# Two mixers of a transformer kernel in another order: pooling last, output tiles in two parts, mask and maximum in one operation

## The reference

```python
h = rms_norm(x, mix_norm[l]) @ w_in[l]              # 1024 -> 2304 columns
u_pool = h[..., OFF_POOL:OFF_MOBA]                  # 256 columns
qm, km, vm = split(h[..., OFF_MOBA:OFF_DIL], 3)     # 4 heads of 64 each
qd, kd, vd = split(h[..., OFF_DIL:OFF_CONV], 3)     # 4 heads of 64 each
u_conv = h[..., OFF_CONV:]
y_pool = pool_mixer(u_pool, pool_w[l], pool_scale[l])  # means over 2, 4, 8, 16 tokens, less the token
y_moba = moba_attention(rope(qm), rope(km), vm)     # 256 tokens are one block: causal attention
y_dil  = dilated_attention(rope(qd), rope(kd), vd)
y_conv = conv_module(u_conv, ...)                   # gate, 31 taps by channel, layer norm, silu
x = x + concat([y_pool, y_moba, y_dil, y_conv]) @ w_out[l]
```

## Time and profile before

| | before |
|---|---|
| median of 3 runs | 1927.93 us (1921.69 to 1929.28) |
| the profiled execution | 1923.98 us |
| its span, first to last instruction | 1922.2 us |
| TensorE busy (PE) | 1884.9 us, 98% |
| VectorE busy (DVE) | 1281.9 us, 67% |
| ScalarE busy (ACT) | 916.0 us, 48% |
| GpSimd busy (POOL) | 247.9 us, 13% |
| DMA | 323.78 MB, mean 168 GB/s |
| mean granted TensorE clock | 0.995 of full speed |
| share of the chain that ended last | PE 78%, DVE 14%, ACT 4% |

### The profile page before, as it was taken

How to read it: one execution, slowest core, us unless ns; L and a number is a source line. 1 busy time by engine, 2 the same in 40 slices (tenths; PEclk the granted TensorE clock), 3 DMA queues, 4 the chain that set the end, 5 groups by cost and what they waited for, 6 DMA issues and landing times.

```text
span 1922.2 us, 28534 instructions
## 1 busy us (share of the span) xinstructions
PE 1884.9 (98%) x11790; PEld 1621.2 (84%) x11790; DVE 1281.9 (67%) x1666; ACT 916.0 (48%) x1288; POOL 247.9 (13%) x175
## 2 busy tenths in 40 slices
PE   9999999999999999999999999999999999979998
PEld 7888969887888888888889878988888889679997
DVE  6776796776677669777664564755554367857774
ACT  5334565334533555633464265533333255855554
POOL 0000007732757600000000110000000000000000
PEclk9999999999999999999999999999999999989999
DMA  8675436776577643776452221323223223025552
GB/s 312 254 272 210 176 135 244 278 264 222 204 270 271 229 162 108 269 281 245 154 187 88 110 78 67 110 88 121 88 88 110 91 85 132 12 88 176 176 197 88
DMA packets 50960, 323.78 MB, mean 168 GB/s; under 512 B 5472, under 2 KB 9744, under 8 KB 12816
## 3 DMA queue, kind: packets, MB, share of 16 engines
q1 hardware_dynamic: 39024, 270.09, 38.9%
q10 hardware_dynamic: 10080, 39.28, 5.4%
q0 software_dynamic: 1728, 12.58, 1.7%
HBM read 320.86 MB, written 1.07 MB: 167 GB/s over the span
## 4 chain that ended last, share of the span: by engine, by line
PE 78%; DVE 14%; ACT 4%; issue 2%; DMA 0%; ACTq 0%; DVEq 0%; SPq 0%
PE ps L558 76%; DVE s_wl L1948 5%; DVE s_tmp L2047 3%; ACT s_wh L1275 2%; DVE s_xx L1948 2%; DVE s_big L2247 1%; PE ps L917 1%; DVE s_tmp L2065 1%; PE ps L774 0%; PE ps L751 0%; DMA s_raw<-in_ffn_gate 0%; ACT s_big L1447 0%; DVE s_big L2070 0%; DVE s_tmp L2469 0%; DVE s_X L2445 0%
## 5 line engine op out<-in xcount | busy, mean ns | idle before, releaser
L558 PE MATMUL ps<-s_xx,s_wh 128*128 128x512 f32 (+1 forms) x3328 | 894.0, 347 | 1.4 <-DVE s_wl L2018 0.6
L1948 DVE TENSOR_TENSOR s_wl<-s_raw,s_wh 128x2048 fp32r<-128x2048 f32 x213 | 493.6, 2319 | 287.7 <-ACT s_wh L1275 287.7
L558 PE MATMUL ps<-s_xx,s_wl 128*128 128x256 f32 (+1 forms) x2208 | 668.6, 303 | 0.4 <-DVE s_xx L2472 0.4
L558 PEld LDWEIGHTS ps<-s_xx,s_wh 128*128 128x128 f32 x3328 | 579.9, 190 | 88.6 <-issue 5.7
L1275 ACT ACTIVATE s_wh<-s_raw 128x2048 fp32r<-128x2048 f32 x213 | 403.7, 1906 | 112.8 <-PE ps L558 108.0
L558 PEld LDWEIGHTS ps<-s_xx,s_wl 128*128 128x128 f32 x2208 | 419.0, 190 | 18.8 <-issue 2.7
L558 PE MATMUL ps<-s_wh,s_hl 128*128 128x512 f32 (+1 forms) x608 | 232.6, 383 | 2.9 <-DVE s_tmp L2047 2.4
L558 PE MATMUL ps<-s_wh,s_hh 128*128 128x512 f32 (+1 forms) x608 | 230.3, 379 | 0.0
L558 PE MATMUL ps<-s_wl,s_hh 128*128 128x512 f32 (+1 forms) x608 | 230.3, 379 | 0.0
L558 PE MATMUL ps<-s_wh,s_xx 128*128 128x256 f32 x928 | 179.2, 287 | 0.0
L1391 ACT ACTIVATE s_tmp<-s_tmp 128x512 f32<-128x512 f32 x44 | 27.8, 632 | 299.8 <-DVE s_tmp L2065 299.8
(11 more groups left out here) (239 smaller groups left out, 1852.3 us busy)
## 6 DMA issues: line engine op xcount, KB each, us to landing
s_raw<-in_ffn_down SPq DMA_DIRECT2D x44, 1024.0 KB, 4.7
s_raw<-in_w_up SPq DMA_DIRECT2D x44, 1024.0 KB, 4.7
s_raw<-in_ffn_gate SPq DMA_DIRECT2D x43, 1024.0 KB, 4.8
s_raw<-in_ffn_up SPq DMA_DIRECT2D x43, 1024.0 KB, 4.8
s_big<-in_w_ada ACTq DMA_DIRECT2D x34, 1024.0 KB, 5.9
s_raw<-in_w_down SPq DMA_DIRECT2D x22, 1024.0 KB, 4.7
s_raw<-in_w_in SPq DMA_DIRECT2D x18, 1024.0 KB, 4.9
s_X<-in_w_ada POOLq DMA_DIRECT2D x12, 1024.0 KB, 7.2
```

The lines of the kernel that those rows point to most:

```text
L558: return pe.matmul(o, lhsT, rhs, start=start, stop=stop, skip_group_check=True)
L1948: dve.tensor_tensor(wide(wl, u), raw[:, u % SLOTS, :].rearrange("p (k n) -> p k n", k=8), f32(wide(wh, u)), SUB).then_inc(*w_low.tick(u))
```

## The change

The pooling unit `w_in` 0 is loaded and multiplied last of the nine projections instead of third, with the work of three head pairs inside it. The running means of the pooling mixer (`windows`) leave the stretch of the taps and are cut into `pool_in`, `windows_first` and `windows_rest`; `pool()` comes after the heads' parts of three output tiles. Output tiles 0, 1 and 2 are multiplied first by the rows of the heads (k = 4, 5, 2, 3) into three banks of their own, later by the rest (6, 7, 0, 1); tile 3 stays whole. Masks are multiplied by 8 once on GpSimd, so that mask, scale and row maximum are one call on VectorE (the sign is turned, hence a minimum and a scale of -1.0 in the exponentials). The table of banks follows, and GpSimd's `row_sum` waits for the pool's products because they share a place.

```diff
-                out += [("w_in", 9 * l + j) for j in (7, 8, 0, 4, 5, 6, 1, 2, 3)]
+                out += [("w_in", 9 * l + j) for j in (7, 8, 4, 5, 6, 1, 2, 3, 0)]
...
-                      ("rope", "km"): 6, "pool": 4, "by token": 0, "back": 1, ("out", 0): 5, ("out", 1): 4, ("out", 2): 5,
+                      ("in", 0): 5, "pool": 5, "by token": 0, "back": 1, ("out", 0): 2, ("out", 1): 3, ("out", 2): 4,
...
-                        "W": (128, 256), "scale": 1.0,
+                        "W": (128, 256), "scale": -1.0,
...
-                project(0, mixed[s, "u"])
+                def out_part(j, ks, last, aside=None):
+
+                    u, b = unit["w_out", 4 * l + j], at["out", j]
+                    if ks[0] == 4:
+                        pe.wait_ge(*w_low[u])
+                        claim(b)
+                    for i in range(2):
+                        if aside and i:
+                            aside()
+                        for n, k in enumerate(ks):
+                            if i == 0:
+                                pe.wait_ge(*mix_in[k])
+                            hi, lo_ = (x[:, 128 * i:128 * i + 128] for x in mix_at(k))
+                            m = mm3(ps[b][:, 256 * i:256 * i + 256], hi, lo_, *w_cols(u, k, 0, 256),
+                                    i == 0 and ks[0] == 4 and n == 0, last and n == len(ks) - 1)
...
-                pool()
-                values(H, 1)
+                project(0, mixed[s, "u"], aside={4: lambda: values(H, 1), 8: lambda: scores(H, 3), 15: lambda: turns(H, 2)})
                 fill()
-                scores(H, 3)
-                turns(H, 2)
+                fill()
                 values(H, 2)
+                turns(H, 3)
                 fill()
-                turns(H, 3)
                 values(H, 3)
-                fill()
                 by_token_()
                 fill()
...
-                for j in range(4):
-                    b = at["out", j]
-                    tokens(unit["w_out", 4 * l + j], [b], [(s, "out", j)], (0, 1), None if j else [[w] for w in mix_in],
-                           not j, {8: lambda j=j: turn(("ffn2", l), j - 1)} if j else {8: back, 12: fill}, source=mix_at)
-                    freed[b] = resid[s, j]
+                heads_in, rest_in = (4, 5, 2, 3), (6, 7, 0, 1)
+                out_part(0, heads_in, False)
+                out_part(1, heads_in, False)
+                back()
+                out_part(2, heads_in, False)
+                fill()
+                pool()
+                out_part(0, rest_in, True)
+                out_part(1, rest_in, True, lambda: turn(("ffn2", l), 0))
+                out_part(2, rest_in, True, lambda: turn(("ffn2", l), 1))
+                tokens(unit["w_out", 4 * l + 3], [at["out", 3]], [(s, "out", 3)], (0, 1),
+                       aside={8: lambda: turn(("ffn2", l), 2)}, source=mix_at)
...
-                        act.wait_ge(*row_max[H.name, h, q if H.banks2(h) else 1])
+                        act.wait_ge(*masked[H.name, h, q])
...
-                                    i = dve.scalar_tensor_tensor(out=e[:, lo:hi], in0=S[:, lo:hi], scalar=0.125, in1=mk,
-                                                                 op0=MUL, op1=ADD)
+                                    dve.wait_ge(*cleared["masks"])
+                                    i = dve.tensor_tensor_reduce(out=e[:, lo:hi], in0=S[:, lo:hi], in1=mk, scale=-0.125,
+                                                                 scalar=3.0e38, op0=ADD, op1=ALU.min,
+                                                                 accum_out=cols(2 * h + q)[:, 0:1])
...
-                windows()
+                conv(4)
                 rope("qm", 0)
                 masks(H, 1)
                 conv(3)
...
                 conv(8)
                 masks(H, 2)
-                conv(3)
-                pool_low()
+                conv(5)
                 over_sums(H, 2)
                 masks(H, 3)
                 out_low(H, 1)
-                conv(7)
+                pool_in()
+                conv(5)
                 over_sums(H, 3)
+                used(1)
+                used(2)
                 conv(62)
-                used(1)
                 out_low(H, 2)
+                used(3)
+                windows_first()
                 out_low(H, 3)
...
-                used(2)
+                windows_rest()
+                used(0)
...
-                used(3)
+                pool_low()
...
+            pool.wait_ge(*cb_in["one"])
+            pool.tensor_scalar(cb[:, 0:1024], cb[:, 0:1024], 8.0, None, MUL).then_inc(*cleared.tick("masks"))
...
+                    pool.wait_ge(*product[("mix", 0), "pool"])
```

More of the change, by code:

```diff
@@ L1006, in mixer @@
                 project(8, mixed[s, "g"], None, {4: lambda: roots(s, 0)})
-                project(0, mixed[s, "u"])
+                mix_in = [mixed[s, "x", 0], mixed[s, "x", 1], x_low[s, "o", 2], x_low[s, "o", 3], x_low[s, "o", 0],
+                          x_low[s, "o", 1], mixed[s, "x", 6], mixed[s, "x", 7]]
+                def out_part(j, ks, last, aside=None):
[12 more added lines that the diff above has]
+                                    i == 0 and ks[0] == 4 and n == 0, last and n == len(ks) - 1)
+                    if last:
+                        m.then_inc(*product.tick((s, "out", j)))
+                        product.also(("unit", u))
+                        freed[b] = resid[s, j]
                 project(4, copied[s, "qd"])
@@ L1518, in mixer @@
                 value(3, "vm")
-                for c in range(2):
-                    act.wait_ge(*product[s, "pool"])
-                    act.activation(mix_at(c)[0], ps[at["pool"]][:, 256 * c:256 * c + 256], ACT.Copy,
-                                   scale=v("pool_scale", 2 * l + c)).then_inc(*x_high.tick((s, "x", c)))
                 exps(H, 2)
+                divide(H, 2)
                 out_high(H, 1)
+                exps(H, 3)
+                turned_out(H, 2)
                 fill()
-                divide(H, 2)
-                turned_out(H, 2)
-                exps(H, 3)
+                divide(H, 3)
                 out_high(H, 2)
-                divide(H, 3)
+                used(2)
+                used(3)
                 fill()
                 turned_out(H, 3)
+                fill()
                 out_high(H, 3)
+                used(0)
                 table_of(ACT.Sqrt)
-                fill()
-                used(2)
                 for t in range(2):
@@ L1551, in mixer @@
                         *x_high.tick((s, "x", 6 + c)))
-                used(3)
                 fill()
+                for c in range(2):
+                    act.wait_ge(*product[s, "pool"])
+                    act.activation(mix_at(c)[0], ps[at["pool"]][:, 256 * c:256 * c + 256], ACT.Copy,
+                                   scale=v("pool_scale", 2 * l + c)).then_inc(*x_high.tick((s, "x", c)))
                 s2 = ("ffn2", l)
@@ L2139, in masks @@
                         if hd["mask"]:
[L2140 to L2144 removed]
+                            row_max.also((H.name, h, q))
+                            continue
+                        dve.wait_ge(*product[H.name, "s", h, q if H.banks2(h) else 1])
+                        src = H.score(h, q)
                         dve.tensor_reduce(c[:, 0:1], src, AX, ALU.max, negate=True).then_inc(
@@ L2225, in mixer @@
                 low_after(unit["w_in", 9 * l + 8])
-                dve.wait_ge(*product[s, "in", 0])
-                if l:
-                    dve.wait_ge(*product[("mix", 0), "pool"])
-                dve.tensor_tensor(U[:, :, 16:272], pair(ps[at["in", 0]][:, :]), both(Rb), MUL).then_inc(
-                    *mixed.tick((s, "u")))
                 dve.wait_ge(*gated[s, "g"])
@@ L2254, in rope, with pool_in, windows_first @@
                     rope_pair((s, n), (s, "rope", n), T(t), at["rope", n], qk[n], cosR, sinR, T(2), (s, n))
-                def windows():
-                    cnt = pair(one("invcnt"))
-                    a, z = slice(0, 64), slice(64, 128)
+                a, z = slice(0, 64), slice(64, 128)
+                def pool_in():
+                    dve.wait_ge(*product[s, "in", 0])
+                    if l:
+                        dve.wait_ge(*product[("mix", 0), "pool"])
+                    dve.tensor_tensor(U[:, :, 16:272], pair(ps[at["in", 0]][:, :]), both(Rb), MUL).then_inc(
+                        *mixed.tick((s, "u")))
+                def windows_first():
                     dve.wait_ge(*cleared["u", l])
@@ L2268, in windows, with windows_rest @@
                         *mixed.tick((s, "w4", 0)))
-                    conv(1)
+                def windows_rest():
+                    cnt = pair(one("invcnt"))
                     dve.wait_ge(*mixed[s, "w4", 1])
                     dve.tensor_tensor(W1[:, 1, 7:272], W2[:, 1, 7:272], W2[:, 1, 3:268], ADD).then_inc(*mixed.tick((s, "w8")))
-                    conv(1)
```

23 lines of the change are left out of this document (7 added, 16 removed).

## The result

The changed kernel takes 1942.98 us (median of 6 runs, 1940.92 to 1944.76), the kernel before in the same comparison 1925.01 us (1921.69 to 1929.28). The ratio is 1.0092, with a 95% interval of 1.0079 to 1.0105: slower by 0.8 to 1.05%, some 18 us. The forecast was +11.4 us. The profiled execution took 1940.92 us with a span of 1939.1, against 1923.98 and 1922.2.

The account below looks back on a forecast made before the run. VectorE was taken to set the length where the mixer loses time. First mixer +5.65 and second +4.2, together +9.85, plus +1.6 for the clock, made +11.4 us on 1927.93: median 1939.3, range 1929 to 1948.

Parts of the forecast that it names:

- The moment c: End of the last convolution tap on VectorE, which by-token waits for: 284.7 in the old first mixer.
- The gain of 0.7 us: First mixer, up to the last tap: its end moves from 284.7 to 283.9 to 284.0.
- the cover: VectorE's wait for `project(0)` at `pool_in()`, 4.3 us even with masks as dear as before, hiding what the masks cost.
- the -4.2 us bound: Fused masks on VectorE, per mixer: the saving if the accumulator read costs nothing; the other bound was -1.2 us.
- the turn: TensorE's wait inside output tile 2, where the turn needs the second residual sum: 0.9 us.
- The wait for `out_low(3)`: TensorE in output tile 0 needs head pair 3 at c+2.6 and gets it at c+4.4: 1.8 us.
- The step that failed: Second mixer: last tap ends at 777.7, gate tile starts at 811.7 against 807.5, +4.2 us.
- c': The last tap's end in the new order, `project(0)`'s end plus 12.2 us of VectorE queue.
- The term of +1.6: Clock: a slow phase reaching into half tile 2 costs about 1.6 us, half of it counted in each mixer.
- the +6.6 end: Clock: the far end, full slow phases paid in each mixer.
- (a): Rival: TensorE's idle time in the taps' stretch is really filled in both mixers, -9 us, 1919; 6 in 100.
- (b): Rival: no change, 1928, as TensorE's work covers VectorE's behind the last tap; 24 in 100 for -5 to +5.
- (c): Rival: the clock at its far end or ada loads late too, +16 to +18 us, 1945; 12 in 100.

Follow-up runs that it names:

- the high part earlier: The changed kernel with ScalarE's `used(2)`, output tile 0's high part in the second mixer, moved ahead of the fill and `divide(H, 3)`: 1940.84 us, ratio 1.0073.
- Whole tiles: The changed kernel with back, fill and pool products first, then output tiles 0 to 3 each over all eight rows instead of halves: 1953.34 us, ratio 1.0136.
- both: The changed kernel with the high part earlier on ScalarE and the other tail order on VectorE: 1931.42 us, ratio 1.0032.
- the other tail order: The changed kernel with VectorE doing both `out_low`, tile 1's low part, layer norm and tile 2's low part before all windows: 1937.71 us, ratio 1.0060.

## Why the prediction was right, and where it was off

**The moment c.** `pool_in()`'s wait and the last tap were forecast for 271.7 and 283.9 to 284.0; the rows show 272.06 and 284.05. The gain of 0.7 us is there. That the masks are worth nothing that the times can tell in this order is shown by the run with the masks apart. But the cover was thinner than forecast: with masks as dear as before VectorE was to stand 4.3 us for `project(0)` and stood 2.00, because it had stood 3.38 us for ScalarE's exponentials on the way. Their own size lay near the cheap end: 1.11 us for a pair of heads, four pairs per mixer, so 4.0 us saved against the -4.2 us bound.

**Behind c, first mixer.** Forecast: `out_low(3)` ready at c+4.4, tile 2's low part at c+11.9, first gate tile's turn at 320.8. Found: 288.7 (c+4.7), 296.8 (c+12.8), 322.73. The wait for the low part was 2.4 in the forecast and is 2.66; the pooling rows 0.7 and 0.74; the turn 0.9 and 1.12. The wait for `out_low(3)`, 1.8 in the forecast, doesn't show in the changed kernel's first mixer, where the slow fill takes its place, and is 0.32 us in the second; the run with the high part earlier has it with 1.85. The missing 1.9 us are sizes. About 0.5 is VectorE's window operations, longer beside GpSimd (0.86 against 0.69 us for L2309), 0.4 is operations rounded down, and 1.0 lies from tile 2 to the gate turn, 25.87 us for 24.85: a half tile is 3.06 us and not 2.9, and there are four of them, and the turn's wait is 0.2 longer.

**The step that failed** is "Second: `project(0)` ends at 762.24 + 3.2 = 765.4, c' = 777.7": the same 12.2 us of queue were put behind `project(0)` in both mixers, with the low part in it at 2.2 us and ready when VectorE comes. In the second mixer the work order gives that slot (`used(2)`) to output tile 0, whose high part ScalarE makes late; I read VectorE's queue and not the one that feeds it. That cost 4.22 us of wait, and c' is 3.9 us later than 777.7 + 7.6 = 785.3. With the sizes of the first mixer's kind (0.4 and 1.0), 3.9 + 1.4 + 4.2 gives the 9.5 us found. The run with the high part earlier takes the wait away.

**The clock.** The term of +1.6 was not there. The slow phases fell ahead of c+11.9, where the prediction said they cost nothing (windows of the changed kernel, columns as above):

```profile
284.90:286.90 2.00, 2.00 (x18) 0.73 (x17) 2.00 (x2) 1.75 (x3) 0.00 (x0) 0.50 0.99 414
286.90:293.90 7.00, 6.93 (x51) 6.72 (x52) 6.45 (x17) 1.97 (x4) 6.61 (x7) 0.90 0.98 348
293.90:296.90 3.00, 0.34 (x4) 0.10 (x2) 3.00 (x3) 1.63 (x4) 3.00 (x2) 1.00 0.03 11
```

The fill runs at 0.50, and at 293.9 TensorE stands for VectorE anyway. Neither the +1.6 nor the +6.6 end came, though the mean granted clock did fall from 0.995 to 0.992. Whole tiles show the case that the term was meant for, and so does "both", with 2.1 us in the first mixer. So 11.4 = 9.85 + 1.6 should have been 9.85 + 1.9 + 5.3 + 0 = 17.0: the sign, the mechanism in both mixers and the range held, one wait was missed, and part of it was made up for by the clock term. That the forecast time (1939.3) lies only 3.7 us from the measured one is partly luck: it started from 1927.93 for the kernel before, which measured 1925.01 in the comparison, and the difference was missed by 6.6 us.

**Rivals.** (a), idle time filled, fell by its own test: VectorE waited 2.37 us at `pool_in()`. Its premise was half right, since 4.35 + 2.37 us of room do appear on VectorE, and the change fills none of it with taps; when they were dealt anew, by-token came at 279.8. (b) asked for tile 2's low part by c+7.7. With the other tail order that happens (291.6 in the first mixer, c+7.6), and the gate turn still comes 3.8 us later than before (318.94): the late windows (1.35) and the two waits of this order (0.74 and 1.12) are not covered, so the condition was not enough. That kernel and its successors lie at +0.2 to 0.6%. (c) named loads for ada; they didn't bind in the changed kernel, but did (4.11 us) as soon as TensorE was early.

## What to carry over

When work is moved behind a wait, read the queue of the engine that feeds each instruction there as well, once for every stage that runs the code: two stages with the same program text can have another tile in the same slot. Time saved on an engine that then waits is worth nothing until something behind the wait is moved ahead of it; here fused masks brought 0.1% (0.2% with three taps earlier) in the old order and nothing that could be told from noise in the new one. And each wait removed should be followed by a look for the next: low part, windows, slow clock, weights' transfer and feed-forward part came up one after the other.

## What the runs showed of the hardware

- A VectorE operation that also reduces (mask, scale, minimum) on 128x128 and 128x256 f32 from PSUM takes 0.28 and 0.42 us, and its accumulator read is a row of its own, 0.08 us, that lies beside the next operation. ScalarE's accumulator read is 0.19 us.
- VectorE's f32 operations on two SBUF operands can be slower while GpSimd works: L2309 took 0.86 us in the first mixer, beside GpSimd's row sums, and 0.69 us in the second, where GpSimd is idle. The Trainium skill ("SBUF — State Buffer", Who interferes with whom) says that a VectorE instruction with two SBUF inputs contends with a GpSimd instruction that reads SBUF. The trace agrees, and shows that either engine can be the one that is slowed: the low part at 294.52 took 2.28 us beside GpSimd, as it does without (2.29 us at 779.84), and the GpSimd operation beside it (294.48, 128x256) took 3.03 us, where the median of its kind is 0.92 us.
- With whole tiles TensorE was busy 7.11 of 15 us, and 6 us at a granted clock of 0.53 followed, while the changed kernel ran at 1.00 in these 6 us: idle time can be paid again in the stretch behind it. A slow phase ahead of a wait for another engine costs nothing (the fill at 284.89 took 1.94 us, 1.07 with the high part earlier, and the gate turns came at 322.73 and 322.79). With the wait gone such a phase is paid (2.1 us in "both", an estimate from its two windows).
